# Two fp32 projections of a two-block layer split into three-pass products, with GpSimd making every low part

## The reference

```python
def merge_branches(o_attn, o_dn, m, w_br_attn, w_br_dn, w_out):
    y = m['gate_attn'] * (o_attn @ w_br_attn) + m['gate_dn'] * (o_dn @ w_br_dn)
    return y @ w_out
...
        x = x + gt1 * merge_branches(o_attn, o_dn, m, w_br_attn[layer], w_br_dn[layer], w_out[layer])
        h2 = rmsnorm(x, norm_ffn[layer]) * (1.0 + sc2) + sh2
        x = x + gt2 * peer_ffn(h2, peer_wq[layer], peer_keys[layer], peer_u[layer], peer_v[layer])
...
        q = (hb @ w_q).reshape(PEER_BLOCK, PEER_HEADS, 2, PEER_KEY_HALF)
        s = jnp.einsum('thpd,hpkd->thpk', q, keys, preferred_element_type=F32)
        half_s, half_i = lax.top_k(s, PEER_TOPK)
```

## Time and profile before

| | us |
|---|---|
| median of 3 runs | 1810.69 (1809.86 to 1812.86) |
| the profiled execution, its own time | 1811.36 |
| its span | 1809.1 |
| output projection, TensorE (L789) | 441.1 to 468.7 |
| query projection and scores (L817, L798, L829) | 468.7 to 506.0 |
| expert loop (L853) from | 506.0 |
| busy over the span: TensorE, VectorE, ScalarE, GpSimd | 98%, 71%, 57%, 9% |

### The profile page before, as it was taken

The page is one execution under the profiler, slowest core; times in us unless marked ns, Lnnn a source line. Parts: engine busy times, 40 slices in busy tenths (PEclk is TensorE's granted clock), DMA queues, the critical chain, the costliest instruction groups (busy, mean ns, idle before and its releaser), DMA issues.

```text
span 1809.1 us, 34619 instructions
## 1 busy us (share of the span) xinstructions
PE 1764.5 (98%) x11840; PEld 1586.5 (88%) x11840; DVE 1276.9 (71%) x2555; ACT 1027.9 (57%) x2070; POOL 162.1 (9%) x136
## 2 busy tenths in 40 slices
PE   7999999999999999999999999999999999999998
PEld 1878799998899988888899999999889899999997
DVE  3786456664398979766766666666686757878887
ACT  2545543341156679766655555555657666666666
POOL 0000004410184520000000000000010000010000
PEclk9999999999999999999999999999999999999999
DMA  8533223234455531255655555555444534555553
GB/s 297 184 103 106 82 83 117 71 112 146 151 177 177 178 108 36 93 195 189 197 185 187 187 188 188 187 188 186 162 174 141 190 127 140 165 184 186 186 186 128
DMA packets 77270, 283.31 MB, mean 157 GB/s; under 512 B 8576, under 2 KB 8576, under 8 KB 76928
## 3 DMA queue, kind: packets, MB, share of 16 engines
q1 hardware_dynamic: 77184, 282.16, 46.7%
HBM read 281.08 MB, written 1.05 MB: 156 GB/s over the span
## 4 chain that ended last, share of the span: by engine, by line
PE 83%; DVE 10%; ACT 3%; issue 1%; DMA 1%; POOL 1%; PEld 0%; PEldq 0%; ACTq 0%; SPq 0%; POOLq 0%; DVEq 0%
PE banks L865 19%; PE banks L853 16%; PE banks L944 9%; PE banks L448 7%; PE banks L1100 7%; PE banks L1124 3%; PE banks L639 2%; PE banks L620 2%; DVE split L2254 2%; DVE arena L2250 2%; PE banks L817 2%; PE banks L789 2%; PE banks L416 1%; PE banks L628 1%; PE banks L958 1%
## 5 line engine op out<-in xcount | busy, mean ns | idle before, releaser
L1412 ACT ACTIVATE split<-arena 128x512 fp32r<-128x512 f32 x492 | 308.9, 629 | 135.0 <-PE banks L853 76.9
L853 PEld LDWEIGHTS banks<-split 128*128 128x128 f32 x2880 | 355.4, 192 | 10.5 <-DVE split L2180 3.1
L865 PE MATMUL banks<-split 128*128 128x512 f32 x1536 | 361.9, 390 | 1.0 <-issue 1.0
L853 PE MATMUL banks<-split 128*128 128x256 f32 x2880 | 358.7, 283 | 3.1 <-DVE split L2180 2.3
L2272 DVE TENSOR_TENSOR split<-arena,split 128x512 fp32r<-128x512 f32 x396 | 270.6, 690 | 105.4 <-ACT split L1412 99.6
L865 PEld LDWEIGHTS banks<-split 128*128 128x128 f32 x1536 | 283.8, 188 | 57.3 <-issue 1.4
L1393 ACT ACTIVATE split<-arena 128x512 fp32r<-128x512 f32 x312 | 194.5, 628 | 125.9 <-PE banks L1100 52.8
L944 PE MATMUL banks<-split 128*128 128x256 f32 x1728 | 217.4, 287 | 4.4 <-DVE split L2350 3.9
L944 PEld LDWEIGHTS banks<-split 128*128 128x128 f32 x1728 | 212.2, 194 | 7.8 <-issue 6.3
L2327 DVE TENSOR_TENSOR split<-arena,split 128x512 fp32r<-128x512 f32 x180 | 123.1, 695 | 66.5 <-ACT split L1393 64.9
L448 PEld LDWEIGHTS banks<-split 128*128 128x128 f32 (+1 forms) x936 | 132.9, 193 | 28.0 <-issue 14.0
(11 more groups left out here) (408 smaller groups left out, 2379.8 us busy)
## 6 DMA issues: line engine op xcount, KB each, us to landing
arena<-wstream SPq DMA_DIRECT2D x525, 512.0 KB, 3.3
arena<-x_t SPq DMA_DIRECT2D x1, 2048.0 KB, 12.0
arena<-matsa SPq DMA_DIRECT2D x1, 1234.0 KB, 6.0
out_t<-arena SPq DMA_DIRECT2D x4, 256.0 KB, 2.0
arena<-mats SPq DMA_DIRECT2D x1, 576.0 KB, 7.8
arena<-crow SPq DMA_DIRECT2D x1, 512.0 KB, 6.8
arena<-rows SPq DMA_DIRECT2D x1, 512.0 KB, 4.0
arena<-mats SPq DMA_DIRECT2D x1, 449.0 KB, 4.2
```

Source lines behind the costliest of these rows:

```text
L853: mm = pe.matmul(ps[:, 4 + b, 0:S], w_parts[:, c, (2 * m + half) % 4, P * k:P * k + P], h_parts[:, e, 4 * half + k, :], start=(half == 0 a ...
L865: mm = pe.matmul(ps[:, 2 * tt + half, :], g_parts[:, e, j % 2, P * tt:P * tt + P], w_parts[:, c, (2 * m + half) % 4, :], start=(first and ...
L1412: act.activation(w_parts[:, 0, (2 * m + half) % 4, :], ring[:, peer_slot(m), 512 * half:512 * half + 512], ACT.Copy).then_inc(sem["w_hi"], 1)
```

## The change

Both projections are made in three passes. A new function `early_parts` on TensorE takes the place of `full` and of the body of `route_product`. Tiles are numbered x = 0 to 15 (0 to 7 output, 8 to 15 query). ScalarE makes the high part of every half (`early_hi`, `early_used`), GpSimd the low part (`early_lo`). The activations are split too: ScalarE writes the high part of `yT` and of the scaled residual (the latter in place of `uT`), and VectorE the low parts (`merged1_lo`, `weighted1_lo`). The query products are 258 columns wide. SyncE frees a ring slot when the low part is made instead of when the product is.

```diff
-            def full(n, src, b, free=None, chunk=None):
-
-                tile_ready(n)
+            def early_parts(x, src, out, n, free=None, chunk=None):
+
                 if free:
                     pe.wait_ge(*free)
...
+                for half in range(2):
+                    pe.wait_ge(sem["in_lo"], HALVES + 2 * x + half + 1)
+                    for k in range(4):
+                        if chunk is not None:
+                            pe.wait_ge(sem["h_lo"], chunk + 4 * half + k + 1)
+                        for c, e in PASSES:
+                            mm = pe.matmul(out, w_parts[:, c, (2 * x + half) % 4, P * k:P * k + P], src[:, e, 4 * half + k, 0:n],
+                                           start=(half == 0 and k == 0 and c + e == 0), stop=(half == 1 and k == 3 and c == 1))
+                    mm.then_inc(sem["tiles_done" if half else "in_used"], 1)
...
+                free = (sem["resid"], 5) if h == 0 else (sem["route_q"], h - 3) if h >= 4 else None
+                early_parts(KT + h, u_parts, ps[:, 4 + h % 4, 0:S + 2], S + 2, free, H_AT["weighted1"] if h == 0 else None)
...
+            def early_used(x, half):
+
+                if half:
+                    act.wait_ge(sem["tiles_done"], N_OUT + x + 1)
+                else:
+                    act.wait_ge(sem["in_used"], 40 + x + 1)
+                early_hi(x + 2, half)
...
+                for half in range(2):
+                    early_used(k, half)
                 act.wait_ge(sem["resid"], k + 1)
-                act.activation(uT[:, k, 0:S], res[:, k, :], ACT.Identity, scale=gain2[:, k:k + 1])
+                act.activation(u_parts[:, 0, k, 0:S], res[:, k, :], ACT.Identity, scale=gain2[:, k:k + 1]).then_inc(sem["h_hi"], 1)
                 act.activation(sq2[:, k, :], res[:, k, :], ACT.Square).then_inc(sem["squares"], 1)
-            roots(1, S)
+            for x in range(KT, 2 * KT - 2):
+                for half in range(2):
+                    early_used(x, half)
+                if x == KT:
+                    roots(1, S)
             act.wait_ge(sem["normed"], 1)
...
+            def weighted1_lo(k):
+                dve.wait_ge(sem["h_hi"], H_AT["weighted1"] + k + 1)
+                dve.scalar_tensor_tensor(u_parts[:, 1, k, 0:S], res[:, k, :], gain2[:, k:k + 1], u_parts[:, 0, k, 0:S].bitcast(F32),
+                                         ALU.mult, ALU.subtract).then_inc(sem["h_lo"], 1)
...
-            add_quads(0, sq2, KT)
+            def early_lo(x, half):
+                pool.wait_ge(sem["in_hi"], HALVES + 2 * x + half + 1)
+                pool.tensor_tensor(w_parts[:, 1, (2 * x + half) % 4, :], ring[:, (N_OUT + x) % RING, 512 * half:512 * half + 512],
+                                   w_parts[:, 0, (2 * x + half) % 4, :].bitcast(F32), ALU.subtract).then_inc(sem["in_lo"], 1)
+
+            pool.wait_ge(sem["in_lo"], HALVES)
+            for x in range(2 * KT):
+                for half in range(2):
+                    early_lo(x, half)
+                if x == KT + 1:
+                    add_quads(0, sq2, KT)
```

More of the change, by code:

```diff
@@ L59 @@
 MATA_AT = dict(zip(MATSA, np.cumsum([0] + list(MATSA.values())).tolist()))
-PARTS_OF = dict(proj=2 * KT, expert=4, in2=KT, rec=4, heads=2, merged2=KT, ff=KT)
+PARTS_OF = dict(proj=2 * KT, merged1=KT, weighted1=KT, expert=4, in2=KT, rec=4, heads=2, merged2=KT, ff=KT)
 H_AT = dict(zip(PARTS_OF, np.cumsum([0] + list(PARTS_OF.values())).tolist()))
@@ L373, in _ @@
             load_freed_by_splits(N_WIN + 3 * RING, N_ADA2 + RING)
-            load_freed_by_matmuls(N_ADA2 + RING, N_PEER + RING)
+            load_freed_by_matmuls(N_ADA2 + RING, N_OUT + RING)
+            for x in range(2 * KT):
+                sp.wait_ge(sem["in_lo"], HALVES + 2 * x + 2)
+                sp.dma_start(tile_at(N_OUT + x + RING), wstream[N_OUT + x + RING]).then_inc(loaded[(N_OUT + x) % RING], 16)
+            for n in range(N_PEER + 2, N_PEER + RING):
+                sp.wait_ge(sem["tiles_done"], n - RING + 1)
+                sp.dma_start(tile_at(n), wstream[n]).then_inc(loaded[n % RING], 16)
             load_freed_by_parts(N_PEER + RING, N_IN2 + RING, M_PEER)
@@ L778, in _ @@
                 branch_dn(d)
-            def full(n, src, b, free=None, chunk=None):
-                tile_ready(n)
+            def early_parts(x, src, out, n, free=None, chunk=None):
                 if free:
                     pe.wait_ge(*free)
[L785 to L790, removed]
+                for half in range(2):
[7 more added lines that the diff above has]
+                    mm.then_inc(sem["tiles_done" if half else "in_used"], 1)
             for d in range(KT):
-                full(N_OUT + d, yT, 4 + d % 4, (sem["resid"], d - 3) if d >= 4 else None, 0 if d == 0 else None)
+                early_parts(d, h_parts, ps[:, 4 + d % 4, 0:S], S, (sem["resid"], d - 3) if d >= 4 else (sem["merged"], d + 5) if d < 2 else None,
+                            H_AT["merged1"] if d == 0 else None)
             def sum_quads(r, src, b):
@@ L1379, in _, with early_hi @@
             phase_end(act, 2)
+            def early_hi(x, half):
+                n = N_OUT + x
+                act.wait_ge(loaded[n % RING], 16 * (n // RING + 1))
+                act.activation(w_parts[:, 0, (2 * x + half) % 4, :], ring[:, n % RING, 512 * half:512 * half + 512], ACT.Copy).then_inc(
+                    sem["in_hi"], 1)
+            def early_used(x, half):
[4 more added lines that the diff above has]
+                early_hi(x + 2, half)
+            for d in range(KT):
+                act.wait_ge(sem["merged"], d + 1)
+                act.activation(h_parts[:, 0, d, :], yT[:, d, :], ACT.Copy).then_inc(sem["h_hi"], 1)
+                if d in (3, 5):
+                    for half in range(2):
+                        early_hi(d // 4, half)
             for k in range(KT):
+                for half in range(2):
+                    early_used(k, half)
                 act.wait_ge(sem["resid"], k + 1)
-                act.activation(uT[:, k, 0:S], res[:, k, :], ACT.Identity, scale=gain2[:, k:k + 1])
+                act.activation(u_parts[:, 0, k, 0:S], res[:, k, :], ACT.Identity, scale=gain2[:, k:k + 1]).then_inc(sem["h_hi"], 1)
                 act.activation(sq2[:, k, :], res[:, k, :], ACT.Square).then_inc(sem["squares"], 1)
-            roots(1, S)
+            for x in range(KT, 2 * KT - 2):
[3 more added lines that the diff above has]
+                    roots(1, S)
             act.wait_ge(sem["normed"], 1)
@@ L1405, in _ @@
             for h in range(8):
+                if h == 3:
+                    act.wait_ge(sem["tiles_done"], N_WQ + 8)
                 late_score(h)
@@ L2142, in _ @@
                                          ALU.mult, ALU.add).then_inc(sem["resid"], 1)
+                if d:
+                    weighted1_lo(d - 1)
+            weighted1_lo(KT - 1)
             def route_query(h):
```

20 lines of the change are left out of this document (15 added, 5 removed).

## The result

The changed kernel takes 1814.49 us (median of 13 runs, 1811.52 to 1816.83) against 1811.0 for the kernel before (13 runs). The ratio is 1.0016, with a 95% interval of 1.0009 to 1.0023: slower by 1.6 to 4.2 us. The prediction was 1813.4, in a range of 1804 to 1819. It gave 0.47 to a change that three runs can't tell from none (up to 0.2%) and 0.33 to slower: at 0.16% the change lies inside that band, and only the 13 runs of each kernel show that it is a loss.

The account below looks back on a forecast made before the run. TensorE's own work was taken to bound the kernel. Savings of 9.4 and 0.4 us against 0.6 + 4.3 + 6.0 given back, plus 1.7 for the clock, were put at +2.7, giving 1813.4 us, range 1804 to 1819.

Parts of the forecast that it names:

- The saving: Output and query tiles on TensorE: 2.88 us each in three passes, eight of each saving 9.4 us in all.
- The feed: High and low parts for TensorE: GpSimd needs 1.28 us a half against 1.44 wanted, so it keeps pace.
- The 0.6 us at the start: Start of the output projection: TensorE waits for the split of the last chunk of `yT`, bounds 0 and 1.5.
- The squares: Before tile 9: GpSimd's six additions stand behind its low parts, so TensorE stands still 4.3 us.
- The port: Normalisation: VectorE and GpSimd take turns at the shared SBUF port, making TensorE wait 6.0 us before query tile 6.
- no turns: Rival, normalisation: VectorE's run takes 5.4 us or a little more, loop starts 5.0 us early, 1805.7; chance 0.20.
- keeps the port for the whole run: Rival, normalisation: VectorE shuts GpSimd out 5.4 us, TensorE waits some 4 for low parts, 1811.4; chance 0.10.
- The clock: After TensorE's standstills: lower clock costs 1.7 us, charged once, behind the wait before query tile 6; bounds 0 and 3.4.
- the second wait: TensorE before query tile 6: 6.0 us of standing still until VectorE has query 2 out, bounds 0 to 8.2.
- slower, clearly: Rival: turns cost the full 1.68 us a pair and the first standstill's slow clock delays query 1, 1817; chance 0.25.
- The sum: Whole kernel: +1.0 us at the expert loop's start and +1.7 for the clock, +2.7, giving 1813.4; chance 0.45.

Follow-up runs that it names:

- out_only: Changed kernel, but only the output projection in three passes, query projection as before; 1808.05 us, ratio 0.998 to the kernel before.
- norm_psum: Changed kernel with the normalisation's second input and seven of eight results in PSUM; 1806.58 us, ratio 0.9971 to the kernel before.
- sums_early: Changed kernel with GpSimd adding the squares ahead of tile 9's low parts instead of behind them; 1812.25 us, ratio 1.0002 to the kernel before.
- queries_first: Changed kernel with VectorE moving queries 2 and 3 out before it normalises instead of after; 1809.24 us, ratio 0.9993 to the kernel before.
- busy_wait: Changed kernel with nine thrown-away fp32 matmuls on TensorE before query tile 6; 1812.26 us, ratio 1.0003 to the kernel before.
- norm_psum_b: norm_psum run again unchanged, on one chip with three other kernels; 1805.57 us over 12 runs, ratio 0.9971 to the kernel before.
- psum_early_b: Second run of the changed kernel with both normalisation through PSUM and squares added ahead of tile 9's low parts; 1802.76 us, ratio 0.9951 to the kernel before.

## Why the prediction was right, step by step

- **The saving.** 2.88 us a tile was right: 23.24 / 8 = 2.90 for the output tiles, 2.91 for the last query. `out_only` shows that it becomes time.
- **The feed.** GpSimd's 32 low parts took 1.30 (median) and never held TensorE up; GpSimd was busy for 38.4 of the 45 us from 445 to 490, about the nine tenths foreseen. The 0.6 us at the start didn't come: the chain has no wait before or in the output tiles.
- **The squares.** The wait and its cause were right, and the size nearly so. The sum let 5.2 us pass between tile 8's end and tile 9's start, 0.86 of it the products with ones, which left 4.3. Measured are 4.8 (466.7 to 471.51), by the same count 4.0; the profile shows only 2.90 as idle because the two products fill 1.92. Two errors lie behind this. The low part ahead of the additions I let end 3.0 us after tile 7, and it ended 2.0 after it (463.7 to 465.7), for GpSimd had no half left over; and the second product with ones took 0.5 us more at the low clock. The additions took 4.5 us, as summed.
- **The port.** The mechanism of the decisive step, one instruction each in turn, is confirmed by `norm_psum`, and by `sums_early` in its length: 1.44 us against my 1.5. The eight took 11.6 us against 12.1; the eight tensor_scalars, which I let run free at 2.2, took 3.1, since GpSimd had nine low parts left and not eight, and the last ended at 490.2. Counted from the first output product, query tile 6 was to start at 493.2 - 441.2 = 52.0 us and started at 493.04 - 440.42 = 52.6. The wait is shorter than the 6.0 of the sum only because TensorE came to it later: tile 13 ended at 47.8 us instead of 46.0, for tile 9 had run at the low clock. That query tile 6 started within 0.6 us of the forecast is in part luck, as the next item shows. The rivals "no turns" and "keeps the port for the whole run" are out.
- **The clock.** This is the term that the sum had wrong. One loss of 1.7 us was charged; there were two. Query tile 6 took 4.85 us, 1.95 over its pace, and tile 9 took 5.13, 2.2 over it, with 0.5 more on the product with ones ahead of it. I wrote that the first loss would be swallowed by the second wait but for what it delays query 1, and then gave that remainder no price in the sum. It had one, for VectorE stood idle until tile 9 ended. Query 1 in the changed kernel:

```profile
476.66 0.16 DVE L2197 COPY arena<-banks 128x1 f32<-128x1 f32 x1 [1.94 <-PE banks L797]
```

The last instruction of query 1 in `queries_first`, where tile 9 ran at the full clock:

```profile
474.81 1.01 DVE L2199 TENSOR_SCALAR arena<-arena 128x256 f32<-128x256 f32 x1
```

Counted from the first output product, query 1 was out at 37.1 us in the changed kernel (477.54 - 440.42) and at 35.6 in the other (475.82 - 440.23). So about 1.5 us of the 2.7 went through, as the rival "slower, clearly" had it for its second half; its first half, 1.68 us a turn, did not come. My sum hid most of that: it had put 2.0 us between tile 9's end and the run, for tensor_scalars that wait for GpSimd. They did wait in `queries_first` (0.77 and 1.01 us), but here, with the late tile, neither did (0.35 each), and it was 0.9.

- **The sum.** The stretch is 68.2 us where 508.7 - 441.2 = 67.5 was summed. By step, against the forecast: 0.5 less up to the start of tile 9, 2.2 more for tile 9, 1.1 less from there to the run, 0.5 less for the turns, 0.9 more for the eight tensor_scalars, 0.4 less for query 2, 0.1 more behind it. Terms of up to 2 us cancel, so that the sum is off by only 0.7 is luck; the path and both waits are not. The sum of 1813.4 was 1.1 under the measured 1814.49; the rest of that is the kernel before, 1811.0 over 13 runs instead of 1810.69 over three.

## What to carry to other kernels

In this kernel, work given to GpSimd was paid for by VectorE's instructions that read two inputs from SBUF, and by its tensor_scalars from SBUF to SBUF: count how many of these are queued in a row while GpSimd has work, and charge each a whole GpSimd instruction. What follows that run in VectorE's queue is what becomes late; moving one input of each instruction to PSUM freed it (here 8 us), and a changed order helped only until the next instruction that someone waited for. A standstill of TensorE can cost the clock behind it, and that loss goes through as far as another engine waits for the slow tile. Before a list of new work is put ahead of an old item on an in-order engine, ask who waits for that item: one step earlier in GpSimd's list was worth 2 to 4 us here.

## What the runs showed of the hardware that was not expected

The granted clock falls during a standstill of TensorE and stays down behind it: 0.70 over the 4.84 us wait, 0.50 in the 3.46 us after it, and back at about 3.9 us after it. With two waits of 1.44 and 1.46 us, which TensorE's ones-products separate, it fell too in the changed kernel's two profiles, in `norm_psum` and `busy_wait`, and in `norm_psum_b`, where it was back within tile 9 (0.75 over 472.04 to 475.50); but in `queries_first`, with the same two waits of 1.44 and 1.46, tile 9 ran at full clock:

```profile
469.20:472.70 3.50, 2.65 (x20) 2.60 (x21) 1.41 (x1) 0.95 (x2) 3.21 (x3) 1.00 0.00 0
```

So a wait of about 3 us in all may or may not cost the clock. That would also make the times of one kernel spread (1803.4 to 1809.7 for `norm_psum_b`, 1802.7 to 1805.0 for `psum_early_b`), which was seen but not shown to be the cause; `psum_early_b` waits only 0.63 and 0.52 us there and kept the full clock in its profile. What decides it is left open.
